# Slot weights inside the gathered token rows, and the end of the expert stage turned token tile by token tile

## The reference

```python
# first block, end
h2 = modulate(rms_norm(x, norm_ffn_g), sh_ffn, sc_ffn).reshape(b * s, d)
y = moe_ffn(h2, w_router, b_router, w_e_gate, w_e_up, w_e_down, w_sh_gate, w_sh_up, w_sh_down)
return x + g_ffn * y.reshape(b, s, d)
...
x = rms_norm(x, final_norm_g)          # after the first block
# second block, beginning
h = jnp.concatenate([meta, x], axis=1)
hn = rmsnorm(h, g_mix)
z = hn @ w_in
```

## Time and profile before

| | |
|---|---|
| median of 3 executions | 3569.56 us (3560.85 to 3582.76) |
| the profiled execution | 3566.24 us, its span 3564.4 us |
| PE busy | 3319.5 us, 93% of the span |
| DVE, ACT, POOL busy | 72%, 51%, 31% |
| mean granted TensorE clock | 0.967 of full speed |

### The profile page before, as it was taken

One profiled execution on the slowest core, in us unless ns is written; L12 is line 12 of the kernel. 1 busy time (PEld: TensorE's weight loads), 2 busy tenths in 40 slices (PEclk: granted clock), 3 DMA queues, 4 the chain that ended last, 5 costly groups with the idle time before them and its releaser, 6 DMA issues. The chain is left out here.

```text
span 3564.4 us, 47063 instructions
## 1 busy us (share of the span) xinstructions
PE 3319.5 (93%) x18017; PEld 2823.4 (79%) x18017; DVE 2552.8 (72%) x3696; ACT 1822.4 (51%) x2490; POOL 1115.7 (31%) x665
## 2 busy tenths in 40 slices
PE   7999789799999999995997899999999999899999
PEld 4987568577877878784876677889999998688787
DVE  3453565878988989895344845569988886688786
ACT  3332542578887888886221344333348872233332
POOL 0000300267777787771000000001013334344341
PEclk9999999899999999997998999999999999999999
DMA  5353113477777777785211211236568889999996
GB/s 193 130 173 115 52 54 102 182 255 247 257 251 249 252 244 259 250 269 166 83 59 40 76 36 60 101 133 227 187 232 314 338 334 399 361 377 373 357 369 226
DMA packets 259679, 747.02 MB, mean 210 GB/s; under 512 B 52640, under 2 KB 112816, under 8 KB 225024
## 3 DMA queue, kind: packets, MB, share of 16 engines
q1 hardware_dynamic: 178224, 570.77, 44.2%
q0 software_dynamic: 81232, 173.25, 15.0%
HBM read 793.57 MB, written 110.65 MB: 254 GB/s over the span
## 5 line engine op out<-in xcount | busy, mean ns | idle before, releaser
L2022 DVE TENSOR_TENSOR w_lo<-w_raw,w_hi 128x2048 fp32r<-128x2048 f32 x285 | 652.3, 2289 | 103.5 <-ACT w_hi L1872 99.1
L1872 ACT ACTIVATE w_hi<-w_raw 128x2048 fp32r<-128x2048 f32 x288 | 551.5, 1915 | 29.3 <-DMA w_raw<-in_e_w,over_rows 25.2
L3061 POOL DMA_INDIRECT rows<-in_peer_u_rows,row_at x128 | 177.1, 1384 | 1230.9 <-DVE row_at L3237 805.5
L662 DVE TENSOR_TENSOR w_lo<-w,w_hi 128x1024 fp32r<-128x1024 f32 (+5 forms) x142 | 173.4, 1231 | 279.8 <-ACT w_hi L636 278.8
L1530 PE MATMUL ps_peer<-peer_xT_hi,w_hi 128*128 128x384 f32 x1024 | 352.8, 345 | 13.6 <-DVE w_lo L3152 13.5
L3152 DVE TENSOR_TENSOR w_lo<-w_raw,w_hi 128x2048 fp32r<-128x2048 f32 x128 | 293.0, 2289 | 98.5 <-ACT w_hi L3072 97.9
L2214 PE MATMUL ps_gu<-w_hi,h2T_hi 128*128 128x512 f32 x792 | 321.6, 406 | 26.7 <-DVE w_lo L2022 24.2
L1532 PE MATMUL ps_peer<-peer_xT_hi,w_lo 128*128 128x384 f32 x1024 | 343.5, 335 | 0.0
L1531 PE MATMUL ps_peer<-peer_xT_lo,w_hi 128*128 128x384 f32 x1024 | 343.5, 335 | 0.0
L636 ACT ACTIVATE w_hi<-w 128x1024 fp32r<-128x1024 f32 (+5 forms) x142 | 149.7, 1063 | 350.2 <-DMA w<-in_w_in 228.3
L1530 PE MATMUL ps_peer<-w_hi,coef_hi 128*128 128x512 f32 x768 | 301.6, 393 | 24.6 <-DVE w_lo L3152 22.5
(11 more groups left out here) (546 smaller groups left out, 8281.6 us busy)
## 6 DMA issues: line engine op xcount, KB each, us to landing
w_raw<-in_e_w SPq DMA_DIRECT2D x195, 1024.0 KB, 6.4
w_raw<-in_peer_u SPq DMA_DIRECT2D x64, 1024.0 KB, 6.0
w_raw<-in_peer_v SPq DMA_DIRECT2D x64, 1024.0 KB, 9.2
w<-in_w_in SPq DMA_DIRECT2D x60, 512.0 KB, 4.8
acts<-act_out SPq DMA_DIRECT2D x64, 384.0 KB, 6.6
gates<-gate_tile SPq DMA_DIRECT2D x6, 4096.0 KB, 17.1
gates_back<-gates SPq DMA_DIRECT2D x16, 1536.0 KB, 15.4
act_back<-acts SPq DMA_DIRECT2D x64, 384.0 KB, 10.7
```

Of the source, the lines that this page charges most:

```text
L1872: nc.scalar.activation(w_hi[:, slot(n), :], w_raw[:, slot(n), :], ACT.Copy).then_inc(hi_done.sem, 1)
L2022: nc.vector.tensor_tensor(w_lo[:, slot(n), :], w_raw[:, slot(n), :], w_hi[:, slot(n), :].bitcast(F32), ALU.subtract).then_inc(lo_done.sem, 1)
L3061: nc.gpsimd.indirect_dma_start(out=row(i), out_offset=None, in_=src, in_offset=bass.IndirectOffsetOnAxis(ap=row_at[:, which, k:k + 1], axi ...
```

## The change

Two parts.

1. **Slot weights.** The normalised scores of a token (64 columns, zero where the expert wasn't taken) are stored behind its 1024 columns in the DRAM copy `h2_rows`, which becomes 1088 wide. The gather of token rows fetches 4352 bytes a row and so brings the weight of a base block along: column 1024 + expert. DVE copies that column (128x1) into `wslot` just ahead of x_low. The 64 indirect gathers of slot weights for base blocks go; the 31 for over blocks stay. Since DVE now reads `xb` too, `take_rows` waits for x_low as well as for the turning on PE.
2. **End of the stage.** The meta rows are loaded, normalised and turned ahead of the token tiles. POOL multiplies tiles 1 to 3 by the gate row, and makes the final x of all four tiles, which nothing in the stage waits for. Both mean squares of a tile come from x and from x times the final gain, so their roots are taken together. PE turns each tile as soon as it is normalised, into banks of PSUM that the stage already holds, and DVE (ACT for the last half tile) copies it to `hT` with the gain. The first weights of the second mixer are fetched in the stage, and the separate `turn` with its boundary goes.

```diff
@@ take_weights, take_rows, the slot weight @@
             def take_weights(b):
-                r = at_row[b - T]
+                if b not in over_blocks:
+                    return
+                r, i = at_row[b - T], over_blocks.index(b)
...
             sp.wait_ge(rows_out.sem, KD)
-            sp.dma_start(scratch["h2_rows"].rearrange("(t p) d -> p t d", p=P), h2r[:]).then_inc(rows_kept.sem, 16)
+            sp.dma_start(scratch["h2_rows"][:, 0:D].rearrange("(t p) d -> p t d", p=P), h2r[:]).then_inc(rows_kept.sem, 16)
+            sp.wait_ge(route_dve.sem, step["flag"])
+            sp.dma_start(scratch["h2_rows"][:, D:D + E].rearrange("(t p) e -> p t e", p=P), sc[:]) \
+                .then_inc(rows_kept.sem, 16)
...
-                if b >= T + 1 and b + 3 < NB:
+                if b >= T + 1 and b + 3 in over_blocks:
                     pool.wait_ge(out_done.sem, 2 * b)
                     take_weights(b + 3)
                 if b + 7 < NB:
                     pool.wait_ge(x_turned.sem, b + 3 - T + 1)
+                    pool.wait_ge(xT_lo_done.sem, b + 3 - T + 1)
                     take_rows(b + 7)
...
             def x_low(b):
                 dve.wait_ge(xT_hi_done.sem, b - T + 1)
                 at = slice(b % 4 * P, (b % 4 + 1) * P)
+                if b not in over_blocks:
+                    r = at_row[b - T]
+                    nc.vector.tensor_copy(wslot[:, r:r + 1], xb[:, b % 4, D + r:D + r + 1])
@@ end of the stage, POOL @@
+            for t in pool_rows:
+                pool.wait_ge(part_in[t].sem, b_part[t] + 16)
+                nc.gpsimd.tensor_tensor(rows[:, t, :], rows[:, t, :], gate_row[:], ALU.mult).then_inc(pool_lo_done.sem, 1)
+            for t in range(T):
+                pool.wait_ge(inverted.sem, t + 2)
+                nc.gpsimd.tensor_tensor(x[:, t, :], rows[:, t, :], stat[:, 3, 2 * t:2 * t + 1].to_broadcast([P, D]),
+                                        ALU.mult)
@@ end of the stage, ACT @@
             square(META_AT)
+            root(T)
+            scale(T)
             square(0)
             square(1)
+            square(2)
             root(0)
-            root(META_AT)
-            square(2)
+            square(3)
+            scale(0)
+            square(4)
             root(1)
...
@@ end of the stage, DVE @@
+            def turned_out(t, halves=(0, 1)):
+                dve.wait_ge(turned.sem, b_turn + 2 + t)
+                for half in halves:
+                    k = slice(4 * half, 4 * half + 4)
+                    nc.vector.tensor_tensor(hT[:, k, t * P:(t + 1) * P],
+                                            turned_bank(t, half).rearrange("p (k t) -> p k t", k=4),
+                                            mix_gain[:, k].unsqueeze(2).to_broadcast([P, 4, P]), ALU.mult)
...
+            gated(0)
             add(0)
+            with_gain(0)
             add(1)
+            with_gain(1)
             variance(0)
             add(2)
             inverse(0)
+            with_gain(2)
             variance(1)
             add(3)
             inverse(1)
+            with_gain(3)
+            turned_out(0)
             variance(2)
+            inverse(2)
+            scale(2)
+            turned_out(1)
             variance(3)
             inverse(3)
+            turned_out(2)
+            turned_out(3, (0,))
@@ end of the stage, PE @@
+            for t in range(T):
+                pe.wait_ge(normed.sem, b_norm + t + 2)
+                if t == 2:
+                    pe.wait_ge(meta_out.sem, b_meta + 1)
+                for k in range(KD):
+                    last = nc.tensor.transpose(turned_bank(t, k // 4)[:, k % 4 * P:(k % 4 + 1) * P],
+                                               xn[:, t, k * P:(k + 1) * P], ident[:])
+                last.then_inc(turned.sem, 1)
@@ second mixer @@
-    turn(core, jobs, [(ret_tab[:], a["k_rope_ret"]), (zeta[:], a["k_zeta"])],
-         lambda sp: ring.begin(sp, [dram_rows(a["w_in_2"], 0, QL), dram_rows(a["w_in_2"], QL, QL + KVL + MROPE)]))
+    ckv, ret_tab, zeta, hT, ring = keep["mixer_2"]
```

More of the change, by code:

```diff
@@ L1601, in experts @@
     core.drop(keep["gate_mix_row"])
+    xb = core.alias(x, "token_rows_in", [P, 4, D + E], F32)
+    core.hold(x, xb)
     order = routed_blocks()
+    over_blocks = [T + i for i, (kind, _) in enumerate(order) if kind == "over"]
     at_row = [o[1] if o[0] == "base" else E + o[1] for o in order]
@@ L1743, in unit_used @@
             eng.wait_ge(dn_mm.sem, 2 * b + 2)
+    core.drop(w_raw, w_hi, x_hi, h2, brow, wr, wr_hi, ones, scT, rank, flag, excl, so, lists, val, vtab, tok,
+              widx, sg, hid, h_hi, h_lo, ob, best, total, mask, wk, pick, wslot, sc, sel, rt, stat)
+    ckv = core.sb("c_kv", [P, T + 1, KVL + MROPE])
+    ret_tab = core.sb("ret_rope", [P, 2, T + 1, 32])
+    zeta = core.sb("zeta", [P, 2, RH])
+    core.hold(w_raw, hT)
+    ring = Ring(core, KD * 512)
+    keep["mixer_2"] = (ckv, ret_tab, zeta, hT, ring)
     with (core.psum("ps_x", [P, D], F32) as ps_x, core.psum("ps_gu", [P, 2, 2 * FF], F32) as ps_gu,
@@ L1849, in _ @@
                 pool.wait_ge(x_turned.sem, b - T + 1)
+                pool.wait_ge(xT_lo_done.sem, b - T + 1)
                 take_rows(b + 4)
@@ new lines, in square, with root @@
+                nc.scalar.activation(junk[r, :] if i == META_AT else xn[:, t, :],
+                                     meta if i == META_AT else (rows if i % 2 else x)[:, t, :], ACT.Square,
+                                     scale=D ** -0.5, accum_out=stat[r, 0, i:i + 1]).then_inc(squared.sem, 1)
+            def root(t):
+                at = slice(2 * t, min(2 * t + 2, META_AT + 1))
+                act.wait_ge(varied.sem, b_var + 2 + (0 if t == T else t + 1))
+                nc.scalar.activation(stat[:, 2, at], stat[:, 1, at], ACT.Sqrt).then_inc(rooted.sem, 1)
@@ L2006, in _ @@
-            scale(0)
-            root(T + 1)
-            square(T + 3)
-            scale(1)
-            root(T + 2)
-            scale(2)
-            root(T + 3)
             scale(3)
-            scale(T)
+            act.wait_ge(turned.sem, b_turn + 1 + T)
+            for k in range(4, KD):
+                nc.scalar.activation(hT[:, k, (T - 1) * P:T * P], turned_bank(T - 1, 1)[:, (k - 4) * P:(k - 3) * P],
+                                     ACT.Copy, scale=mix_gain[:, k:k + 1])
         @block.vector
```

178 lines of the change are left out of this document (91 added, 87 removed).

## The result

| | before | changed |
|---|---|---|
| median, 10 executions each on one chip | 3567.04 us (3554.36 to 3582.76) | 3581.38 us (3571.80 to 3593.99) |
| ratio to before | | 1.0045, 95% interval 1.0028 to 1.0061 |
| span of the profiled execution | 3564.4 us | 3579.3 us |
| 2nd to 92nd routed output | 871.40 us | 886.33 us |
| first gate multiply to the next stage's first split | 33.67 us | 34.20 us |

I had forecast 3530, in a range of 3514 to 3560. The result lies outside, on the other side of no change.

The account below looks back on a forecast made before the run. PE, busy 93%, was taken as the bound, with 33.5 us of loop stalls fed by POOL's backlog. From 3566.2, minus 29 (loop) and 8 (end of stage), came 3529, written as 3530 us; range 3514 to 3560.

Parts of the forecast that it names:

- Added on POOL: Routed-block loop: the row gather's new wait for x_low(b+3) costs 0, being met or nearly met when the gather is due.
- Put, queued behind it, waits for the output anyhow: Routed-block loop, POOL's queue: put behind the waiting row gather loses nothing, since it must wait for the block's output; 0.
- Rival C: Loop: the new wait keeps POOL late, with a 6.75 us stall every sixth block; +73 - 8, 3631 us; chance 0.05.
- Removed: 64 gathers, -29: Loop: dropping 64 slot-weight gathers frees 116 us of POOL's time, so most of 33.5 us of stalls go; -29 us.
- Rival A: Loop: scatter landings feed the stalls, not POOL's instructions; half stay (-16), 3542, chance 0.17; all stay, 3558, chance 0.12.
- Added on DVE: 64 copies at 0: Loop: 64 copies of 128x1 fit in DVE's 0.67 us idle time per block; 0, or 11 us without that cover.
- End of the stage, -8: End of the expert stage: 11 us less without contention, 2 to 3 us lost to contention; -8 us taken.
- The sum without contention: End of the stage: DVE, ACT and PE steps added from 1654.7 reach the next stage at 1677, not 1688.3; -11 us.
- the price of contention: End of the stage: POOL's three gate multiplies each stretch by one DVE operation (1.2 us), losing 2 to 3 us.
- Rival B: End of the stage: DVE and POOL wholly take turns, so it gains nothing or loses 5; 3537 to 3542 us; chance 0.12.
- B's signs: End of the stage: POOL's multiplies take well over 3.5 us each, and DVE stands idle ahead of its adds.

Follow-up runs that it names:

- e10: Changed kernel with its wait kept, but put(b) and the third over unit issued ahead of the row gather on POOL; ratio 0.9957 to the kernel before, loop 855.37 us.
- e4: Changed kernel, but DVE copies block b+3's slot weight first in block b and the row gather waits for that copy, not x_low; ratio 0.9941 to the kernel before.
- e8: Changed kernel with the slot weight copied first in the block and no POOL multiply at the stage's end; ratio 0.9898 to the kernel before, median 3528.08 us.
- e9: Changed kernel, DVE's copy still just ahead of x_low but with its own signal, which releases the row gather instead of x_low; ratio 0.9941 to the kernel before.
- e1: Kernel before with only the added wait of the row gather for x_low, all slot-weight gathers kept; ratio 1.0135 to the kernel before, loop 913.01 us.
- e7: Changed kernel with no POOL multiply at the stage's end: DVE makes the gates, ACT the final x; ratio 1.0025 to the kernel before, end 26.02 us.
- e5: Changed kernel, but DVE makes all four gate multiplies and POOL keeps the final x; ratio 1.0044 to the kernel before, end 31.78 us.
- e6: Changed kernel, but ACT makes the four final x multiplies and POOL keeps the three gates; ratio 1.0036 to the kernel before, end 28.67 us.

## Why the prediction was wrong

DVE behind the x_low of the earlier trace rows, in the kernel before:

```profile
1104.18 2.29 DVE L2022 TENSOR_TENSOR w_lo<-w_raw,w_hi 128x2048 fp32r<-128x2048 f32 x1 [0.57 <-ACT w_hi L1872]
```

- **The step that failed is "Added on POOL": the wait for x_low at 0.** It measures +35 to +42 us. I took its price from the earlier trace rows, one gather that was issued 0.27 us behind x_low and took 0.99. That row was from the block after a stall: there DVE had waited 1.09 us for ACT ahead of x_low, and w_lo followed it only at 1104.18, 0.3 us after the gather had started (the row above). In an undisturbed block w_lo follows x_low at once (890.06), the gather starts inside it and takes 2.35. The row showed the operation in a state in which it isn't hurt; 58 of the 87 row gathers of before start inside a w_lo.
- *Put, queued behind it, waits for the output anyhow.* This was the second half of the step, and e10 shows it false: what stands behind the gather starts late because of it (put 2.3 to 7.8 us behind its output in the rows of the result), and with put ahead of the gather the same wait costs next to nothing.
- **Rival C named the mechanism, and its price and chance were off.** It had the gather caught by w_lo, put slipping, the stall in every sixth block, and the point of decision at 7.8 us behind; the stalls of the changed kernel come in just this rhythm, 15 of them. But they are of 2.4 us on average (35.5 / 15), not 6.75, and against them stands what the removal brings. I gave C 0.05 on the strength of that one gather.
- *Removed: 64 gathers, -29.* Right in sign, and of the right order once the wait is harmless: -20, -30, -21 and -16 (e4, e8, e9, e10), with 6 to 10 us of play in each. In the changed kernel the lighter load of POOL shows only against e1, which has the wait and all gathers (643.55 us busy from 800 to 1600); against the kernel before, the instructions that were left took the time up (611.88 and 615.56).
- *Rival A, the landings feed the stalls.* Its stronger form, that the removed gathers do nothing, is refuted by the same runs. Its weaker form, half of the stalls stay (-16), is not excluded by the loop times. Against it stands e9: POOL waits 86.9 us for scatters, more than the 83.0 before, and PE waits for w_lo only 6.5 us.
- *Added on DVE: 64 copies at 0.* In the changed kernel a copy takes 0.14 to 0.16 us, and an undisturbed block still needs 9.31 us (899.23 and 908.54). Right.
- **End of the stage, -8: measured +0.5.** The sum without contention came out right in total, in part by luck: it gave 22.3 us (1677 - 1654.7), and e7, with three gate multiplies of 1.22 put back on DVE, takes 26.0 against 22.3 + 3.7 = 26.0; but e7 also has ACT's final multiplies ahead of the last root, for which DVE waits 1.84 us and which the sum did not have, so the sum was too long elsewhere by about as much. What failed is the price of contention, 2 to 3 us, and a term that the sum did not have, POOL's drain. On the gate multiplies the two engines take turns whole: DVE's three operations beside them take 3.25 + 3.37 + 3.25 = 9.87 us, so (9.87 - 3.66) / 3 = 2.07 us of each belong to a POOL multiply, and from POOL's side (9.93 - 3.66) / 3 = 2.09. The nearest multiply without such company, the last final one, takes 1.89. But in the forecast I had priced the turns only on the gate multiplies. The four final multiplies, "which nothing in the stage waits for", cost more, 5.5 of 8.2 us: they hold DVE's small operations, and they are the last thing ahead of POOL's drain, for which the boundary waits.
- *Rival B, DVE and POOL take turns,* holds for DVE's operations, and its "gains nothing" came true. But the wait at the boundary, 3.8 of the 5.5 us, was in no rival, and neither of B's signs appeared as written: POOL's multiplies take 3.31 us each, not over 3.5, and DVE's operations are listed longer instead of DVE standing idle.

The Trainium skill, page "SBUF — State Buffer", section "Summary: rules for kernel authors", says that when DVE has two SBUF inputs while a GpSimd operation reads SBUF, the one that issues second blocks until the first is finished. The end of the stage agrees for the gate multiplies in both directions (DVE 3.37 us instead of 1.22, POOL 3.31 on average where the sum above leaves 2.09 for itself). In the loop the trace agrees for POOL's DMA issues as the second one: they end 0.9 to 1.5 us after the w_lo. As the first one a gather did not hold w_lo back: at 908.59 w_lo began on time and took its 2.29 us.

## What to carry to other kernels

Price a new wait on a queue by the state into which it releases the instruction and by what stands behind it in the queue, not by its length: ask what the releasing engine does in the very next microsecond, and take a row from an undisturbed period, not from the recovery after a stall. Put a waiting instruction behind the urgent one in its queue, or let it go by an earlier signal of its own. And work given to POOL "because nothing waits for it" was waited for twice here: by DVE's operations beside it, and at the next block boundary. Given to ACT it still held the last tile, because it stood ahead of that tile's root.

## What the runs showed of the hardware

- POOL's drain at the end of the expert stage lasts 6.2 us beyond its last multiply in the changed kernel, in e5 and in e6, and 6.18 us in e7, where there is none. At the boundary that `turn` had (L296 of the kernel before) it took 0.03 to 0.04 us each of six times; POOL issued indirect DMAs in the expert stage and none in that one. What it waits for wasn't tried.
- An indirect gather's issue on POOL that takes 1.0 us otherwise ends 0.9 us after the w_lo inside which it starts (the changed kernel's rows at 890.90, 893.56 and 912.17); a scatter's takes 1.6 and ends 1.5 us after it (884.21, 896.49). Started 0.29 us ahead of w_lo, a gather takes 1.03 (e9). x_low, with one of its two inputs in PSUM, does not stretch it: the gather of e9 starts beside it.
- Such a stretched issue cost little where put and the over weights stood ahead of it (e10: 86 of 87 row gathers start inside a w_lo, loop 855.37).
- A DVE operation on 128x1 took 1.67 us beside a POOL multiply, 0.16 without one (changed kernel and e6).
- Forty transposes in `turn` took 8.81 us at a mean granted clock of 0.55 and 7.00 at 0.79 (before and e1).
